# Channel mixer of a decoder step: seven block products for eight in the up projection of 768 tokens, in turns of two pairs

## The reference, cut to what matters

```python
h2 = rms_norm(x, lp['norm_ffn'])
up = jnp.einsum('btd,df->btf', h2, lp['w_up'])            # 1024 -> 2 * 3072, gate and value
up_c, new_ffn_buf = causal_dwconv(up, ffn_buf, lp['ffn_conv_w'], lp['ffn_conv_b'])   # width 3, over tokens
act = jax.nn.gelu(up_c[..., :D_FF]) * up_c[..., D_FF:]
x = x + jnp.einsum('btf,fd->btd', act, lp['w_down'])      # 3072 -> 1024
```

## Time and profile before

| | |
|---|---|
| median of 3 runs | 1940.98 us (1938.55 to 1942.34) |
| profiled execution, first to last instruction (span) | 1936.0 us |
| TensorE busy | 1887.3 us, 97% |
| VectorE busy | 1278.9 us, 66% |
| ScalarE busy | 868.7 us, 45% |
| GpSimd busy | 43.7 us, 2% |
| granted TensorE clock, mean | 0.997 |
| mixer | from 1080 us to the end |

### The profile page before, as it was taken

The page is one execution under the profiler, slowest core; times in us unless marked ns, Lnnn a source line. Parts: engine busy times, 40 slices in busy tenths (PEclk is TensorE's granted clock), DMA queues, the critical chain, the costliest instruction groups (busy, mean ns, idle before and its releaser), DMA issues. The chain is left out here.

```text
span 1936.0 us, 37599 instructions
## 1 busy us (share of the span) xinstructions
PE 1887.3 (97%) x13112; PEld 1712.6 (88%) x13112; DVE 1278.9 (66%) x2835; ACT 868.7 (45%) x1686; POOL 43.7 (2%) x78
## 2 busy tenths in 40 slices
PE   6999999999999999979999999999999999999998
PEld 6999999999999999956665999989898999999896
DVE  6776767676767676875544774748475665748476
ACT  6766657575757474743343431313031322314033
POOL 0000000000000000031100000000000000000000
PEclk9999999999999999989999999999999999999999
DMA  6421211111212122399994220202021111102012
GB/s 200 154 63 50 66 50 59 54 54 52 63 46 64 45 60 72 134 343 370 377 347 164 66 65 24 77 11 77 11 66 33 55 44 45 55 23 76 11 46 105
DMA packets 166409, 182.86 MB, mean 94 GB/s; under 512 B 9542, under 2 KB 138534, under 8 KB 166294
## 3 DMA queue, kind: packets, MB, share of 16 engines
q1 hardware_dynamic: 165081, 180.66, 28.3%
q10 hardware_dynamic: 1212, 0.81, 0.1%
HBM read 162.49 MB, written 24.20 MB: 96 GB/s over the span
## 5 line engine op out<-in xcount | busy, mean ns | idle before, releaser
L1298 PE MATMUL ps<-h_hi,w_hi 128*128 128x384 f32 (+1 forms) x1152 | 386.6, 336 | 5.0 <-DVEq L1013 3.4
L1298 PE MATMUL ps<-h_hi,w_lo 128*128 128x384 f32 (+1 forms) x1152 | 376.5, 327 | 0.0
L1298 PE MATMUL ps<-h_lo,w_hi 128*128 128x384 f32 (+1 forms) x1152 | 376.4, 327 | 0.0
L2432 PE MATMUL ps<-h_hi,f_w_hi 128*128 128x320 f32 (+1 forms) x1136 | 370.7, 326 | 0.8 <-PEq L1587 0.8
L2432 PE MATMUL ps<-h_hi,f_w_lo 128*128 128x320 f32 (+1 forms) x1136 | 370.4, 326 | 0.0
L2432 PE MATMUL ps<-h_lo,f_w_hi 128*128 128x320 f32 (+1 forms) x1136 | 370.2, 326 | 0.0
L2511 ACT ACTIVATE yc<-ps,f_prm 128x384 f32<-128x384 f32 x144 | 93.3, 653 | 556.6 <-PE ps L2432 382.8
L2412 PE MATMUL ps<-d_hi,act 128*128 128x512 f32 x816 | 257.1, 390 | 0.5 <-issue 0.5
L1298 PEld LDWEIGHTS ps<-h_hi,w_hi 128*128 128x128 f32 x1152 | 217.2, 189 | 9.0 <-issue 4.0
L1298 PEld LDWEIGHTS ps<-h_lo,w_hi 128*128 128x128 f32 x1152 | 217.1, 188 | 0.6
L1298 PEld LDWEIGHTS ps<-h_hi,w_lo 128*128 128x128 f32 x1152 | 216.8, 188 | 0.0
(11 more groups left out here) (320 smaller groups left out, 2894.0 us busy)
## 6 DMA issues: line engine op xcount, KB each, us to landing
k<-in_cache_k SPq DMA_DIRECT2D x64, 512.0 KB, 6.5
vr<-in_cache_v SPq DMA_DIRECT2D x60, 512.0 KB, 6.4
w_raw<-in_w_in SPq DMA_DIRECT2D x48, 512.0 KB, 3.9
f_raw<-in_w_up SPq DMA_DIRECT2D x48, 512.0 KB, 3.9
f_raw<-in_w_down SPq DMA_DIRECT2D x24, 512.0 KB, 3.7
bias<-bias_tiles_dram SPq DMA_DIRECT2D x8, 576.0 KB, 3.8
merged_dram<-mg SPq DMA_DIRECT2D x8, 544.0 KB, 2.7
wo_raw<-in_w_out SPq DMA_DIRECT2D x8, 512.0 KB, 5.8
```

The costliest lines, as they stand in the source:

```text
L1298: last_ = pe.matmul(bank(s)[:, 0:n], w[:, W_SLOT[g], k, :], x[:, k, off:off + n], start=(k == 0 and i == 0), stop=(k == KT - 1 and i == 2))
L2432: l_ = pe.matmul(ps[:, e % 6, 0:n], w[:, p, k, :], x[:, k, off:off + n], start=(k == 0 and i == 0), stop=(k == KT - 1 and i == 2))
```

## The change

A pair's first 768 tokens are two chunks of 384, and its product is a 2 by 2 block product: weights `A11`, `A12` (gate block, first and second half of the depth), `A21`, `A22` (value block), tokens `B11`, `B12`, `B21`, `B22`. Strassen's scheme needs seven products of half the depth (12 matmuls each) in place of eight, M1 to M7, of sums of weight blocks (`SUMS`) by sums or differences of token blocks. The third chunk stays as it was (`c2g`, `c2v`). What comes with it:

- **Token sums.** They are made once, in the first turn, whose two pairs are computed without the scheme (`plain`): POOL adds three pairs of blocks for the high and for the low parts (`token_sums`), DVE makes two differences and the whole sums, ACT and DVE split them.
- **Weight sums.** For each pair POOL makes five sums of 512 elements from `f_raw` (`next_sums`), each after the product that used its buffer; ACT rounds them, POOL makes their low parts (`low_sums`), after `states`, which waits for both filters of the pair before. DVE now makes the low parts of the four blocks one by one (`low_block`).
- **Recombination.** ACT copies products M4, M3 and M1 to rows in SBUF (`f_row0` for the gate, `f_row1` for the value), and DVE adds or subtracts the others from PSUM, eight times a pair (`combine`). The filter, the GELU and the product then run over whole rows of 1024 and 64 elements, from **SBUF** (`conv`, `multiply`, `low_part`).
- **Turns.** A turn is two pairs (`GF = 2`, 12 turns). The down projection of a turn stands in the next one behind c2g, c2v, M4 and M3 of its first pair; PSUM banks, buffers and all counts follow. The last pair of all has an order of its own, with its filter in two pieces.
- In other functions only the page table's place is another (`c.words`).

```diff
-GF = 3
+GF = 2
 NG = DFF // 128 // GF
...
+HK = KT // 2
+CH = 384
+BLOCKS = {"A11": (0, 0), "A12": (0, HK), "A21": (1, 0), "A22": (1, HK)}
+SUMS = {"S1": ("A11", "A22", "add"), "S5": ("A11", "A12", "add"), "S7": ("A12", "A22", "subtract"),
+        "S6": ("A21", "A11", "subtract"), "S2": ("A21", "A22", "add")}
+SUM_ORDER = ("S1", "S5", "S7", "S6", "S2")
+LAST_SUM_ORDER = ("S2", "S1", "S5", "S7", "S6")
...
+GROUPS = ("c2g", "c2v", "M4", "M3", "M1", "M5", "M7", "M6", "M2")
...
+ADDS = ("c11m", "c22m", "c12", "c11a", "c11b", "c22b", "c21", "c22e")
...
+            def token_sums():
+
+                for i, (x, y) in enumerate((("B11", "B22"), ("B11", "B12"), ("B21", "B22"))):
+                    for src, dst in ((c.h2_hi, u_sum), (c.h2_lo, v_sum)):
+                        pool.tensor_tensor(dst[:, i, :, :], token(src, x).bitcast(F32), token(src, y).bitcast(F32),
+                                           ALU.add).then_inc(uv_done, 1)
...
+            def states(f, j):
+
+                pool.wait_ge(prm_in[j], 16 * f + 16)
+                for p in range(2):
+                    if not (plain(f) and j == 0):
+                        pool.wait_ge(cv_done, at_conv(*before(f, j), "gv"[p]))
+                    pool.sem_inc(pool_settled, 1)
+                    pool.tensor_copy(samples(p)[:, :, 0:2],
+                                     prm[j][:, p, FCONV_W + 1:FROW].rearrange("p (b t) -> p b t", b=DEC_B))\
+                        .then_inc(state_in, 1)
...
+            def low_sums(f, j):
+
+                for name in (LAST_SUM_ORDER if final(f, j) else SUM_ORDER):
+                    pool.wait_ge(shi_done, at_split(f, j, name))
+                    pool.tensor_tensor(sum_lo(name), sum_at(name), sum_hi(name, final(f, j)).bitcast(F32), ALU.subtract)\
+                        .then_inc(slo_done, 1)
+
+            def next_sums(f, j):
+
+                g, i = after(f, j)
+                for p in range(2):
+                    pool.wait_ge(raw_in[p], 16 * (2 * g + i))
+                for name in SUM_ORDER:
+                    if not plain(f):
+                        pool.wait_ge(pe_done, at_pe(f, j, "M" + name[1]))
+                    x, y, op = SUMS[name]
+                    pool.tensor_tensor(sum_at(name), weight(raw, x), weight(raw, y),
+                                       ALU.add if op == "add" else ALU.subtract).then_inc(sum_done, 1)
...
+                    for name in (LAST_GROUPS if final(f, j) else GROUPS):
+                        if name[0] == "M":
+                            product(f, j, name)
+                        else:
+                            chunk_2(f, j, 0 if name == "c2g" else 1)
+                        if j == 0 and name == "c2g":
+                            pe.wait_ge(stc_done, 4 * GF * f)
+                            pe.wait_ge(add_done, 2 * NT * (f - 1)) if not (isinstance(f, int) and f == 1) else None
+                            turn_states(7)
+                        if j == 0 and name == "M3":
+                            down(f - 1)
...
-            def split_up(f, i, r):
-                dve.wait_ge(whi_done, 2 * GF * f + i + 1)
-                dve.tensor_tensor(w_lo[:, i % 2, :, :], raw[:, (r + 1) % 3, :, :], w_hi[:, i % 2, :, :].bitcast(F32),
-                                  ALU.subtract).then_inc(wlo_done, 1)
...
+            def low_block(f, j, name):
+
+                g, i = after(f, j)
+                dve.wait_ge(phi_done, at_block(g, i, name))
+                dve.wait_ge(pe_done, lo_free(f, j, name))
+                dve.tensor_tensor(weight(w_lo, name), weight(raw, name), weight(w_hi, name).bitcast(F32), ALU.subtract)\
+                   .then_inc(plo_done, 1)
+
+            def low_down(f):
+
+                for j in range(GF):
+                    dve.wait_ge(dhi_done, GF * f + j + 1)
+                    dve.tensor_tensor(d_lo[:, j, :], d_raw[:, j, :], d_hi[:, j, :].bitcast(F32), ALU.subtract)\
+                       .then_inc(dlo_done, 1)
+
+            def combine(f, j, name):
+
+                p, at = int(name[1]) - 1, 2 + CH * (int(name[2]) - 1)
+                out = row[p][:, at:at + CH]
+                product, op, copied = {"c11m": ("M1", ALU.add, "s22"), "c22m": ("M3", ALU.add, "s22"), "c12": ("M5", ALU.add, "s12"), "c11a": ("M5", ALU.subtract, "s11"),
+                                       "c11b": ("M7", ALU.add, "s11"), "c22b": ("M6", ALU.add, "s22"),
+                                       "c21": ("M2", ALU.add, "s21"), "c22e": ("M2", ALU.subtract, "s22")}[name]
+                order = LAST_ADDS if final(f, j) else ADDS
+                earlier = [x for x in order[:order.index(name)] if x[0:3] == name[0:3]]
+                dve.wait_ge(pe_done, at_pe(f, j, product))
+                dve.wait_ge(copy_done, at_copy(f, j, copied))
+                if earlier:
+                    dve.wait_ge(sum_added, at_add(f, j, earlier[-1]))
+                l_ = dve.tensor_tensor(out, out, ps[:, BANK_OF[product], 0:CH], op)
...
+            def conv(f, j, p, t0, t1, sample, piece=""):
+
+                n = "gv"[p]
+                w = [prm[j][:, p, k:k + 1] for k in range(FCONV_W)]
+                y, s = y_prompt(p, j)[:, t0:t1], samples(p)
+                taps_made[0] += 1
+                made = 4 * (2 * f + j) + taps_made[0]
+                dve.wait_ge(y_done, at_row(f, j, n + piece))
+                dve.scalar_tensor_tensor(out=y, in0=row[p][:, 1 + t0:1 + t1], scalar=w[1], in1=y, op0=ALU.mult,
+                                         op1=ALU.add).then_inc(tap_done, 1)
+                if sample:
+                    taps_made[0] += 1
+                    dve.wait_ge(y_done, at_row(f, j, n + "_s"))
+                    dve.wait_ge(state_in, 2 * (2 * f + j) + p + 1)
+                    dve.scalar_tensor_tensor(out=y_sample(p, j), in0=s[:, :, 1:1 + DEC_T], scalar=w[1],
+                                             in1=y_sample(p, j), op0=ALU.mult, op1=ALU.add).then_inc(tap_done, 1)
+                dve.wait_ge(tap_done, made)
+                l_ = dve.scalar_tensor_tensor(out=y, in0=row[p][:, t0:t1], scalar=w[0], in1=y, op0=ALU.mult, op1=ALU.add)
+                if sample:
+                    dve.wait_ge(tap_done, made + 1)
+                    l_ = dve.scalar_tensor_tensor(out=y_sample(p, j), in0=s[:, :, 0:DEC_T], scalar=w[0],
+                                                  in1=y_sample(p, j), op0=ALU.mult, op1=ALU.add)
+                l_.then_inc(cv_done, 1)
```

DVE's queue of one turn reads now (`body`, from its loop over the two pairs):

```diff
+                    taps_made[0] = 0
+                    low_part(*before(f, j), 0, SEQ, True)
+                    if j == 0 and isinstance(f, int) and f == 1:
+                        low_down(0)
+                    low_block(f, j, "A22")
+                    low_block(f, j, "A11")
+                    if j == 0:
                         add(f - 1)
...
+                    for name in ("c11m", "c22m", "c12", "c11a"):
+                        combine(f, j, name)
+                    low_block(f, j, "A12")
+                    if j == 1:
+                        low_down(f)
+                    for name in ("c11b", "c22b"):
+                        combine(f, j, name)
+                    conv(f, j, 0, 0, SEQ, True)
+                    low_block(f, j, "A21")
+                    combine(f, j, "c21")
+                    combine(f, j, "c22e")
+                    conv(f, j, 1, 0, SEQ, True)
+                    multiply(f, j, 0, SEQ, True, "v")
```

More of the change, by code:

```diff
@@ L2274, in mixer, with plain, final @@
-    raws = [s for s in turn if s[0] in ("W", "DW")]
-    NRAW = len(raws)
+    w_prm = c.fprm_dram.rearrange("p (a k r) -> p a k r", a=2, r=FROW)
     def all_turns(eng, body):
         body(0)
-        with eng.Fori(1, NG - 1) as f:
+        body(1)
+        with eng.Fori(2, NG - 1) as f:
             body(f)
         body(NG - 1)
-    def first(f):
+    def plain(f):
         return isinstance(f, int) and f == 0
-    def last_(f):
-        return isinstance(f, int) and f == NG - 1
+    def final(f, j):
+        return isinstance(f, int) and f == NG - 1 and j == GF - 1
@@ L2289, in mixer, with lo_free @@
+    def lo_free(f, j, name):
+        if plain(f):
+            return at_pe(f, j, "c2g" if name[1] == "1" else "c2v")
+        return at_pe(f, j, {"A11": "M3", "A22": "M4", "A12": "M5", "A21": "M6"}[name])
     tiles = [0, 1, 2, 3, 4, 5, NT - 1, 6, 7]
     norms = [0, 1, 2, 3, 4, 5, 6, NT - 1, 7]
-    def down_bank(e):
-        return 2 + e if e < 4 else 6 + e % 2
-    def wait_before(eng, semaphore, f, per, i, back):
-        if not (first(f) and i - back < 0):
-            eng.wait_ge(semaphore, per * f + i - back + 1)
+    END_BANKS = (7, 2, 3, 4, 5, 6)
@@ new lines, in row_free, with copy_chunk @@
+            def row_free(f, j, p):
+                if not (plain(f) and j == 0):
+                    g, i = before(f, j)
+                    act.wait_ge(cv_done, at_conv(g, i, "gv"[p]))
+                    act.wait_ge(stc_done, 4 * (2 * g + i) + 2 * p + 2)
+            def copy_chunk(f, j, name):
```

(29 more changed lines are left out.)

807 lines of the change are left out of this document (523 added, 284 removed).

## The result

The changed kernel takes **2050.98 us** (median of 4 runs, 2049.52 to 2053.19), the kernel before beside it 1940.43: a ratio of 1.0573, 95% interval 1.0558 to 1.0588, so 110.5 us slower. Predicted were 2042, range 1960 to 2080. The profiled span is 2049.5 us, against 1936.0.

What follows compares the result with a forecast made beforehand. PE was taken to bound the mixer as long as every operand is split in time. Terms: -45.9 saved, +104 steady turns, +44 start and end, sum +102 on 1940.98, forecast 2042 us, range 1960 to 2080.

Steps and rivals of the forecast that it cites:

- What goes, 45.9 us: Up projection: seven block products for eight save 12 matmuls, 2.09 us, in each of 22 pairs.
- Prices: Instruction times taken from the earlier trace, such as 1.28 us for POOL's 512-wide sum and 0.69 for DVE's.
- The cost that decides: POOL reading SBUF and DVE reading two SBUF operands exclude each other; each meeting costs DVE about 1.0 us.
- A: PE's stall at the next turn's second chunk product, waiting for DVE's low_block A21: 3.8 us a turn.
- B: PE's stall before the down projection, waiting for low_part of the same pair: 3.5 us a turn.
- C: PE's stall in the second pair, where M6 waits for combine c11a: 2.8 us a turn.
- The steady turns, +104: Three stalls plus 0.3 us at the first pair's chunk product, 10.4 us a turn, ten times: +104 us.
- rival 3: PE's clock drops to half after the stalls, adding up to 39 us: 2060 to 2085 us; chance 0.15.
- Start and end, +44: PE's waits in the first turn (15.7, 9.3 and 7 us) and in the last pair (12): together +44 us.
- Rival 1: Meetings of POOL and DVE cost nothing, so the kernel gets faster: 1927 us; chance 0.14.
- Rival 2: The ports exclude, but the order adapts and only capacity counts: 1960, up to 2015 us; chance 0.14.
- marks named for a right forecast: Fewer matmuls, DVE and POOL means above solo prices, PE idle some 10 us a turn and 25 before 1150.

Runs made afterwards that it cites:

- e3: The changed kernel with product M2 made twice in all 22 pairs, giving PE back 45.9 us of matmuls: 2048.25 us.
- x4: x2 plus the first turn's token sums on DVE and a down projection that waits for the second pair's act only where it reads it: 1932.55 us.
- e7: x4 with product M2 made twice in all 22 pairs, 45.9 us of matmuls: 1966.10 us, 33.6 above x4.
- e1: The changed kernel with POOL's ten weight sums a pair replaced by memsets of the same 512 columns, which read nothing: 1942.2 us.
- x2: e5 with part of POOL's weight sums moved under DVE's adds of the down projection's banks, and two low blocks moved; no arithmetic left out: 1956.11 us.
- e6: The changed kernel with each first pair's product M3 made twice, just ahead of the down projection, 23.0 us more PE work: 2042.93 us.
- e5: The changed kernel with DVE's two low_down of a turn moved, one ahead of each conv, of g and of v: 2044.28 us.

## Why the prediction was right, and where by luck

The sign, the size and the mechanism held: +110.5 measured, +102 forecast. (The terms add up to +102.1 on 1940.98, which is 2043; the 2042 of the prediction is a slip of 1 us.)

- **What goes, 45.9 us.** Right as a count of PE's work. Its worth is another matter: nothing in the changed kernel's setting (e3, -3 us), 33.6 in x4's (e7).
- **Prices.** Right within a few per cent: POOL 1.285 to 1.29 us at 512 (1.28 taken), the combine 0.546 (0.55), DVE alone 0.69 and 1.22 (e1). The estimate worked out from the figure of the Trainium skill (GPSIMD Engine Reference, section Elementwise — side-by-side cycle accounting), 1.31, is 2% above what was measured.
- **The cost that decides.** Right, and shown: e1 takes the readings away and the loss with them, x2 takes the meetings away and leaves the work. The mean wait of about 1.0 us holds where a meeting is certain: 2.236 - 1.22 = 1.02 for the split of act, 1.255 - 0.22 = 1.04 for its 64 columns. For the low block it is 0.67 in the mean, since not every one meets.
- **A, B, C: 3.8, 3.5, 2.8.** Each too large, by 0.2 to 0.5. Undisturbed, the trace has 3.28, 3.25 and 2.29 us, 8.8 together, and 7.5 in the mean of nine turns (A falls to 1.15, B to 1.72, where PE came at the low clock). The path of A had an overlap in conv g; there POOL is idle, and the filter's 1024-wide instructions take their 1.28.
- **The steady turns, +104.** The sum is right by two errors that cancel. A turn is 77.9 us, 10.7 above the 67.2 of PE's work that e7 gives (71.36 - 4.17, my 66.9 and a transpose of 0.3); ten are 107. But of the 10.7 the waits are 7.5. The other 3.2 are in PE's busy time, 70.4. The turn whose clock is 1.00 throughout is busy 68.3, so 1.1 of them come without a low clock (x4, almost without waits, has 67.9), and 2.1 us a turn are low clock, which I had put into rival 3 and left out of the sum.
- **Start and end, +44.** The total less the rest gives 110.5 + 45.9 - 107 = 49. By terms: first wait 15.27 (15.7 forecast), low blocks of the next chunk products 3.99 + 1.02 (9.3: too large), first down 6.56 (7); end 3.60 (3.9), 1.72 for the low sum (3.6), 2.47 (2.7), and none for the last down (1.6). The waits make 35, not 44. Of the 14 us to 49 some 10 are PE's busy time, an estimate: at the prices of the earlier trace rows its matmuls cost 50.3 of the 56.0 us that it is busy from 1082.66 to the first down, and 55.6 of the 59.8 from the last turn's first down at 1946.01 to the last up matmul at 2013.56; behind four of these waits the granted clock is 0.50 to 0.68. Another 2 are the end: from the last up matmul on, the changed kernel takes 35.9 us for a down of 23.6, the kernel before 46.0 for one of 35.4. The rest is open, and no run has isolated these parts. So the 44 came near by luck as well.
- **Rival 1** (meetings cost nothing) is out by every duration. **Rival 2** (the order adapts and only capacity counts, 1960 to 2015) is out by the time itself: the queues are fixed, and each instruction waits where it stands. The order had to be changed by hand: x2 has the same load on both engines and takes 1956 us. **Rival 3** (clock) came true in part: after one or two of a turn's three waits the clock is low, and the slowed PE comes late to the next wait and shortens it. It adds 2.1 us a turn to PE's busy time, but what a turn loses by it is 77.9 - 77.2 = 0.7 us, 7 in ten turns; e6, which fills B, wins back 8.
- **"The reader should not expect the reordered down to hide A and B."** True of the kernel as it is. But "POOL's sums all hang on M1 to M2, outside it" was too strong: those that follow the second pair's products can wait for the down, and that is what x2 does.
- Of the marks named for a right forecast these came: 260 fewer PE instructions, the means above the prices alone, and waits released by f_w_lo, act and f_row, with POOL named once. Two came short: PE is idle 7.5 us a turn, not 10, and 20 us before 1150, not 25.

Open: how much of x4's 6.1 us over before would be left if the kernel before were tuned as long; that it has no idle PE to win from the earlier trace rows speaks for most of it. The 10.4 us in the first turn were not attacked further.

## What to carry to other kernels

Before work is given to an idle GpSimd, list what VectorE does at that time: here each of its instructions with two SBUF operands that met one of GpSimd's waited for the rest of it, even one of 64 columns (1.255 us for 0.22), so the sums belong under VectorE's reads of PSUM. An operation taken from the bounding engine is worth its time only if the others can follow: put it back once (as in e3) and see whether the time moves. When a wait goes, ask which stands behind it (e5), and let a long matmul group wait for each operand where it reads it.

## What the runs showed of the hardware that I had not expected

- GpSimd's copy of 512 columns (0.61 us, one read) excludes VectorE as its two-operand sum (1.29) does; its memset (0.53, no read) meets nothing.
- After some of PE's waits of 2.3 and 3.3 us TensorE's granted clock was 0.50 to 0.72, after others of the same length and place 1.00; more work in such a wait made the kernel faster (e6, 8.1 us), and e3, with 45.9 us more work, has the clock at 0.99 and is not slower. Which of the waits brings the clock down was not found.
- PE's busy time is no measure of its work where it waits: 70.4 us a turn here, 68.3 in a turn at full clock, 67.9 in x4, for the same matmuls.
